# VectorE's part of the Strassen up projections, rotated by part of a turn

## The reference, cut to what matters

```python
def _ffn(h, p):
    return (jax.nn.silu(h @ p['w_ff_gate']) * (h @ p['w_ff_up'])) @ p['w_ff_down']
...
    for l in range(DEPTH_2):
        ...
            xc = _post(xc, _ffn(_modulate(xc, mod_c[3], mod_c[4]), p), mod_c[5], ln2_g[l], ln2_b[l])
        x = _post(x, _latent_mixer(_modulate(x, sh1, sc1), mem, cos, sin, p), g1, ln1_g[l], ln1_b[l])
        x = _post(x, _ffn(_modulate(x, sh2, sc2), p), g2, ln2_g[l], ln2_b[l])
```

## Time and profile before

| what | value |
|---|---|
| median of 3 runs | 3365.79 us (3365.56 to 3367.2) |
| the profiled execution's own time | 3362.28 us |
| its span, first to last instruction | 3360.5 us |
| TensorE busy | 3126.1 us (93%) |
| VectorE busy | 1604.3 us (48%) |
| ScalarE busy | 658.0 us (20%) |
| mean granted TensorE clock | 0.979 of full speed |
| `up2` of layer 0 | about 2023 to 2300 us of the span |
| `up2` of layer 1 | about 3100 to 3265 us of the span |

### The profile page before, as it was taken

One profiled execution on the slowest core, in us unless ns is written; L12 is line 12 of the kernel. 1 busy time (PEld: TensorE's weight loads), 2 busy tenths in 40 slices (PEclk: granted clock), 3 DMA queues, 4 the chain that ended last, 5 costly groups with the idle time before them and its releaser, 6 DMA issues. The chain is left out here.

```text
span 3360.5 us, 40681 instructions
## 1 busy us (share of the span) xinstructions
PE 3126.1 (93%) x13452; PEld 2269.3 (68%) x13452; DVE 1604.3 (48%) x3329; ACT 658.0 (20%) x1603; POOL 52.2 (2%) x101
## 2 busy tenths in 40 slices
PE   7999899989978999999999989999989999998998
PEld 5888788878864555654444437885446677887887
DVE  4356126636663356765554134432134556754551
ACT  2334210000003333310002022110043331022111
POOL 0000001100010000000000000000000000000000
PEclk9999899999989999999999999999999999999999
DMA  4242347746661011112221111222211122433442
GB/s 156 89 146 103 126 150 268 262 154 227 237 226 50 2 71 47 56 50 75 75 76 68 62 50 63 87 87 88 81 41 53 56 70 94 150 113 113 145 151 103
DMA packets 104574, 363.09 MB, mean 108 GB/s; under 512 B 11200, under 2 KB 17344, under 8 KB 104256
## 3 DMA queue, kind: packets, MB, share of 16 engines
q1 hardware_dynamic: 90416, 310.92, 26.5%
q0 software_dynamic: 14096, 51.39, 4.3%
HBM read 361.21 MB, written 1.05 MB: 108 GB/s over the span
## 5 line engine op out<-in xcount | busy, mean ns | idle before, releaser
L490 PE MATMUL bank<-H,W 128*128 128x256 f32 (+1 forms) x3600 | 988.7, 432 | 13.3 <-DVEq L273 10.8
L490 PEld LDWEIGHTS bank<-H,W 128*128 128x128 f32 x3600 | 687.3, 192 | 296.0 <-issue 218.3
L490 PE MATMUL bank<-YG,W 128*128 128x256 f32 (+1 forms) x2336 | 675.5, 447 | 11.1 <-ACTq L273 11.1
L490 PEld LDWEIGHTS bank<-YG,W 128*128 128x128 f32 x2336 | 444.0, 190 | 231.5 <-issue 189.3
L705 PE MATMUL bank<-MX,SQ 128*128 128x256 f32 (+1 forms) x1056 | 184.7, 332 | 17.8 <-DVE SQ L1675 15.5
L705 PEld LDWEIGHTS bank<-MX,SQ 128*128 128x128 f32 x1056 | 162.7, 192 | 38.1 <-issue 10.2
L1933 DVE SCALAR_TENSOR_TENSOR YG<-WORK,PR,YG 128x512 f32 (+1 forms) x240 | 147.0, 612 | 0.0
L1610 DVE TENSOR_SCALAR WORK<-bank,MOD 128x256 f32<-128x256 f32 x48 | 21.7, 480 | 258.6 <-PE bank L490 258.6
L995 ACT ACT_TABLE_LOAD x20 | 25.7, 1283 | 585.8 <-DVEq L273 584.6
L1933 DVE SCALAR_TENSOR_TENSOR WORK<-WORK,PR 128x512 f32<-128x512 f32 (+1 forms) x224 | 137.2, 612 | 0.0
L1540 DVE SCALAR_TENSOR_TENSOR WORK<-WORK,MX 128x1024 f32<-128x1024 f32 x96 | 117.4, 1223 | 38.1 <-DMA WORK<-ada 32.3
(11 more groups left out here) (286 smaller groups left out, 3396.4 us busy)
## 6 DMA issues: line engine op xcount, KB each, us to landing
W<-stream SPq DMA_DIRECT2D x556, 512.0 KB, 3.3
WORK<-ada POOLq DMA_DIRECT2D x96, 512.0 KB, 4.0
W<-stream SPq DMA_DIRECT2D x24, 384.0 KB, 3.2
W<-stream SPq DMA_DIRECT2D x16, 128.0 KB, 2.4
CN<-consts SPq DMA_DIRECT2D x1, 1984.0 KB, 11.3
PR<-params SPq DMA_DIRECT2D x1, 1303.5 KB, 9.6
X<-x_in SPq DMA_DIRECT2D x1, 1024.0 KB, 5.8
MX<-mem_in SPq DMA_DIRECT2D x1, 1024.0 KB, 8.1
```

Source lines behind the costliest of these rows:

```text
L490: m = pe.matmul(out_ap, W[u][:, c, :], src[:, c, cols], start=first and c == 0, stop=last and c == k - 1)
```

## The change

VectorE's loop over the 11 turns becomes a first part, a loop of 10 turns, and a last part. The first part makes the weight sums and `first` of turn 0. A turn of the loop then makes corner, left and cross of the current turn, and after that, for each j, the weight sums of the *next* turn, `right_hidden` of the current one, and `first` of the next one. The last part makes corner, left, cross and right of turn 10. No arithmetic is added or removed; the queues of TensorE, ScalarE and SyncE keep their order.

```diff
+                    if isinstance(body, tuple):
+                        begin, body, end = body
+                        begin(Step(tally, plan, number, 0, counting=False))
+                        with engine.Fori(0, turns - 1) as turn:
+                            body(Step(tally, plan, number, turn), Step(tally, plan, number, turn + 1))
+                        end(Step(tally, plan, number, turns - 1, counting=False))
...
-                for j in range(2):
-                    sum_weights(j)
-                    first(j)
-                for j in range(2):
-                    corner(j)
-                left_hidden(0)
-                cross(0)
-                left_hidden(1)
-                cross(1)
-                for j in range(2):
-                    right_hidden(j)
...
+            def up2_begin(s):
                 for j in range(2):
-                    sum_weights(j)
-                    first(j)
+                    sum_weights(s, j)
+                    first(s, j)
+
+            def up2(s, following):
+                up2_middle(s)
+                for j in range(2):
+                    sum_weights(following, j)
+                    right_hidden(s, j)
+                    first(following, j)
+
+            def up2_end(s):
+                up2_middle(s)
                 for j in range(2):
-                    right_hidden(j)
+                    right_hidden(s, j)
```

More of the change, by code:

```diff
@@ L128, with __init__ @@
 class Step:
-    def __init__(self, tally, plan, number, turn):
+    def __init__(self, tally, plan, number, turn, counting=True):
         self.tally, self.plan, self.number, self.turn = tally, plan, number, turn
+        self.counting = counting
         self.made = {}
@@ L174, in tick @@
         self.made[name] = self.made.get(name, 0) + 1
-        row = self.tally.seen.setdefault(name, {})
-        row[self.number] = row.get(self.number, 0) + 1
+        if self.counting:
+            row = self.tally.seen.setdefault(name, {})
+            row[self.number] = row.get(self.number, 0) + 1
         return self.tally.sem(name), self.unit(name)
@@ L267, in run @@
                 if body is not None:
-                    if turns == 1:
+                    if isinstance(body, tuple):
[4 more added lines that the diff above has]
+                        end(Step(tally, plan, number, turns - 1, counting=False))
+                    elif turns == 1:
                         body(Step(tally, plan, number, 0))
@@ L1670, in sum_hidden, with add, sum_weights @@
                 dve.scalar_tensor_tensor(t[3], t[1], -1.0, b21, ALU.mult, ALU.subtract).then_inc(made, 1)
-            def up2(s):
+            def add(o, a, b):
+                return dve.tensor_tensor(o, a, b, ALU.add)
+            def sum_weights(s, j):
+                a, b = W[j], W[2 + j]
+                made = f"w_summed{j}"
+                dve.wait_ge(*s.done(f"loaded{j}"))
+                dve.wait_ge(*s.done(f"loaded{2 + j}"))
+                dve.wait_ge(*s.before(f"c12{j}"))
+                add(w_sum[j][0], b[:, EVEN, :], b[:, ODD, :]).then_inc(*s.tick(made))
+                add(w_sum[j][2], a[:, EVEN, :], b[:, EVEN, :]).then_inc(*s.tick(made))
+                dve.wait_ge(*s.done(made))
+                add(w_sum[j][1], w_sum[j][0], a[:, EVEN, :]).then_inc(*s.tick(made))
+                dve.wait_ge(*s.done(made, 2))
+                add(w_sum[j][3], w_sum[j][1], a[:, ODD, :]).then_inc(*s.tick(made))
@@ new lines, in first, with gated @@
+            def first(s, j):
+                n = (T2 - first_column(s.layer)) // 2
+                dve.wait_ge(*s.done(f"p2{j}"))
+                dve.wait_ge(*s.done(f"p1_held{j}"))
+                add(up_c[:, j, 0:n], held[j][:, 0, 0:n], bank[3 * j + 1][:, 0:n]).then_inc(*s.tick(f"first_taken{j}"))
+            def gated(s, j, half):
+                n = (T2 - first_column(s.layer)) // 2
+                c = up_c[:, j, half * n:(half + 1) * n]
+                dve.wait_ge(*s.done(f"gate_sig{j}", half))
+                link(s, dve.tensor_tensor(c, c, up_s[:, j, half * n:(half + 1) * n], ALU.mult))
+                return c
@@ L1673, in up2, with right_hidden, up2_middle @@
+            def right_hidden(s, j):
+                n = (T2 - first_column(s.layer)) // 2
+                c = gated(s, j, 1)
+                dve.wait_ge(*s.done(f"corner_taken{j}"))
+                dve.scalar_tensor_tensor(G[:, s.turn * 2 + j, T2 - n:T2], c, -1.0, held[j][:, 3, 0:n], ALU.mult, ALU.mult)                   .then_inc(*s.tick(f"hidden{j}"))
+            def up2_middle(s):
                 c0 = first_column(s.layer)
                 n = (T2 - c0) // 2
-                add = lambda o, a, b: dve.tensor_tensor(o, a, b, ALU.add)
@@ L1698, in corner @@
                     add(held[j][:, 3, 0:n], held[j][:, 2, 0:n], bank[3 * j + 2][:, 0:n]).then_inc(*s.tick(f"corner_taken{j}"))
[L1700 to L1707, removed]
+                for j in range(2):
+                    c = gated(s, j, 0)
                     dve.wait_ge(*s.done("unit", 2 + j))
-                    dve.scalar_tensor_tensor(G[:, s.turn * 2 + j, c0:c0 + n], c, -1.0, bank[3 * j][:, 0:n], ALU.mult, ALU.mult)\
-                       .then_inc(*s.tick(f"left_hidden{j}"))
-                def cross(j):
+                    dve.scalar_tensor_tensor(G[:, s.turn * 2 + j, c0:c0 + n], c, -1.0, bank[3 * j][:, 0:n], ALU.mult, ALU.mult)                       .then_inc(*s.tick(f"left_hidden{j}"))
                     dve.wait_ge(*s.done(f"c12{j}"))
                     add(up_c[:, j, n:2 * n], held[j][:, 1, 0:n], bank[3 * j + 2][:, 0:n]).then_inc(*s.tick(f"cross_taken{j}"))
[L1716 to L1720, removed]
+            def up2_begin(s):
                 for j in range(2):
-                    sum_weights(j)
-                    first(j)
+                    sum_weights(s, j)
+                    first(s, j)
+            def up2(s, following):
+                up2_middle(s)
                 for j in range(2):
-                    corner(j)
-                left_hidden(0)
-                cross(0)
-                left_hidden(1)
-                cross(1)
+                    sum_weights(following, j)
[3 more added lines that the diff above has]
+                up2_middle(s)
                 for j in range(2):
-                    right_hidden(j)
+                    right_hidden(s, j)
             def modulation(s):
@@ L1953, in _ @@
                       "attend": attend, "gla": gla, "conv": conv, "conv_norm": layernorm, "merge2": merge2,
[L1954 removed]
+                      "out2": out2, "post_mixer": layernorm, "ln_ffn": layernorm, "up2": (up2_begin, up2, up2_end), "down2": down2,
                       "post_ffn": layernorm},
```

## The result

The changed kernel takes 3382.08 us (median of 5 runs, 3380.08 to 3397.03) against 3365.79 us, a ratio of 1.0057 with a 95% interval of 1.0036 to 1.0078: slower by 16 us, where 10 us were forecast, and 1 us above the range. The profiled execution took 3387.73 us (span 3385.9).

The account below looks back on a forecast made before the run. TensorE, busy 93% of the span, was taken as the bound, waiting in layer 1 for VectorE's weight sums. Ten turns at +1.01 us gave +10.1 us on 3365.79: 3375.9 us, 8-in-10 range 3367.5 to 3381.

Parts of the forecast that it names:

- Which loop pays, and by which circle: Layer 0 loses nothing; layer 1 pays, by a 14.54 us circle from `third(0)` through `cross(1)` and `first(1)` back.
- The same work stays in the circle: On VectorE in layer 1, both `right_hidden`, 1.28 us a turn, stay ahead of `first(1)`.
- The sums meet the slot's load: In layer 1 the sums wait for W[2], landing after 4.08 us on average; 2.7 us of advance over ten turns.
- rival 1: In layer 1 W[2] lands before `cross(1)` is done; gain up to 3.8 us, 3362.0 us; chance 0.04.
- The sum of +10.1 us: Layer 1: sums 0.27 us earlier, 1.28 us of `right_hidden` behind them, +1.01 us a turn, 10 times.
- The circle: Layer 1's chain from `third(0)` to `cross(1)`, 6.56 us, to `first(1)`, 7.14 us, and back to `third(0)`, 0.84 us.
- What shows at TensorE: In layer 1 the first gap shrinks by about 0.3 us; the later two grow to about 1.7 and 1.1 us.
- The loop's turn: On VectorE in layer 1, the 0.38 us for the loop to go round leave the path from `cross(1)` to `first(1)`.
- The clock: TensorE's clock in layer 1: no clock drop was counted in the sum; drops were left to rival 3.
- rival 3: Longer gaps in layer 1 pull TensorE's clock down once a turn, adding 8 us: 3384 us; chance 0.06.

Follow-up runs that it names:

- layer1_only: The changed kernel with only layer 1's loop rotated, layer 0's in the order of before: 3392.50 us against 3368.43, ratio 1.0065.
- layer0_only: The changed kernel with only layer 0's loop rotated, layer 1's in the order of before: 3374.83 us against 3368.43, ratio 1.0019.
- act_order: The kernel before with ScalarE's copy after second(0) put ahead of the sigmoid of j = 1: 3364.14 us against 3365.86, ratio 0.9991.
- dose3: The kernel before with three extra additions ahead of the weight sums in each turn of layer 1: 3381.37 us against 3367.98, ratio 1.0033.
- right_last: The changed kernel with both `right_hidden` moved behind `first(1)` of the next turn: 3365.38 us against 3368.43, ratio 0.9990.
- after_short: The changed kernel with layer 1's W[2] loads cut to 128 columns from turn 1 on: 3363.38 us against 3368.43, ratio 0.9991.
- right_first: The changed kernel with both `right_hidden` directly behind cross(1), ahead of the next turn's sums: 3368.00 us against 3365.86, ratio 1.0001.
- the two later timings: The changed kernel timed again, unaltered, 3391.69 us against 3367.98, and `layer1_only`, 3392.50 us against 3368.43.
- dose6: The kernel before with six extra additions ahead of the weight sums in each turn of layer 1: 3400.44 us against 3367.98, ratio 1.0089.

## Why the prediction was right in its sum and wrong in its range

- **Which loop pays, and by which circle: right.** Layer 0 keeps 24.17 us a turn; `layer1_only` carries the whole loss (`layer0_only` has a small one of its own, 6.4 us, of which the profile shows 2.4 and none in layer 0). `act_order` confirms that `third(0)` waited by way of `first(1)`, and `dose3` shows that the part from `cross(1)` to `first(1)` is paid in full.
- **"The same work stays in the circle": right.** Moving `right_hidden` off it (`right_last`) takes the loss away.
- **"The sums meet the slot's load": right.** VectorE waits for W in all ten rotated turns, by 0.48 to 1.50 us. `after_short` shows rival 1's condition: with the load early the change is a small gain.
- **The sum of +10.1 us: right in size.** The circle cost 8.1 and 10.8 us in the two profiles. The slot landed after 3.93 and 4.22 us on average; I had 4.08.
- **What shows at TensorE: right.** Gaps of about 1.7 and 1.1 us were forecast from the ends of issue; by the profile's idle times 0.77 and 0.21 us became 1.42 and 0.85.
- **The loop's turn, 0.38 us: half as large.** `right_first` gained 0.18 us.
- **The clock: the step that failed.** I set rival 3 aside because TensorE stood idle for half of a 3 us window in layer 1's first turn and the clock was at 1.00 there, gave it 0.06 and left its 3384 us out of the range, so the sum had nothing for the clock. The drops came, 3, 7 and 5 of them in three profiles, 4.9 to 10.1 us in all. One window without a drop was no evidence for ten turns whose gaps lie otherwise. Rival 3 had priced one drop a turn at 0.8 us; a drop costs 1.4 to 1.6 us and comes in about half of the turns, which gives about the same 8 us by luck. 10.1 + 4.9 to 10.1 us is 3381 to 3386, and the first timing, 3382, lies there. How many drops the executions without a profile had is not known, and the two later timings are 24 us over before, 4 to 6 us more than the circle's 10.1 and the drops in their profiles; these few microseconds stay open. The Trainium skill, "TensorE: Matmul & The Clock Gate", section "HAM oscillation", describes a clock that falls again and again in a loop with a repeated wait. I noted that the trace of before showed none of it; the rows of after show it, at 4.57 us against 2.94 for the same 24 instructions, though in 3, 7 and 5 of the turns of three profiles and not each time round.
- The rule of the Trainium skill, "DMA: Bandwidth & Descriptors", section "Rules for kernel authors", to wait late for a transfer, agrees with the loss here. But `right_last` waits as early and loses nothing: what counted was the work put between the wait and `first(1)`. By the fit in the Trainium skill, "DMA: Bandwidth & Descriptors", section "Anatomy of one DMA", made for the GpSimd path, 512 KB come to an estimated 3.2 us. W[2], issued by SyncE among two other loads, took 3.3 to 4.5 us in the two profiles of the changed kernel; W[0], which no other load of weights overlaps, took 3.1 to 3.4 us.

## What to carry to other kernels

When an operation is moved behind a later one on the same queue, ask what it used to hide: here two operations that nobody waited for filled the wait for a weight slot, and moved past it they delayed those that TensorE waits for. Such a filler belongs behind the last operation that others wait for, or ahead of the wait, never between the wait and that operation. And where a change lengthens TensorE's pauses in a loop, keep a clock drop in the range, for each turn that has the pauses, even if the old trace shows a pause that went unpunished.

## What the runs showed of the hardware that I had not expected

- The clock drops are not the same from one execution to the next: the same kernel had 3 in one profile and 7 in another, and the unchanged kernel's spans differ by 11.5 us outside the loops that were studied (3194.4 and 3205.5 us).
- A low clock costs only what falls outside TensorE's waits. In `dose6` the 16 instructions that took 2.49 instead of 2.05 us ran into a wait for VectorE and cost nothing, the 32 behind them cost 0.49 us a turn. In the changed kernel a drop fell on 24 instructions with no wait behind them and cost its full 1.4 to 1.6 us.
- The same VectorE instructions in the same order took 0.23 us a turn more in one build (`layer0_only`). Its cause stays open.
